# Splitting the next stage's first weights before, rather than after, the last chunk of a feed-forward block

## The reference

```
x = x + 0.5 * swiglu(rmsnorm(x, ffn1_norm), gate1, up1, down1)     # feed-forward, 2816 wide
x = x + concat([mixer(h), memory_cross_attention(h, mem)]) @ w_out  # h = rmsnorm(x, mix_norm)
x = x + 0.5 * swiglu(rmsnorm(x, ffn2_norm), gate2, up2, down2)

def swiglu(h, w_gate, w_up, w_down):
    return (jax.nn.silu(h @ w_gate) * (h @ w_up)) @ w_down
```

## Time and profile before

| | |
|---|---|
| median of three runs | 2265.5 us |
| the profiled execution: its time, its span | 2264.19 us, 2262.4 us |
| PE busy | 1807.7 us (80%) |
| DVE busy | 796.6 us (35%) |
| ACT busy | 604.1 us (27%) |
| HBM read | 601.81 MB, 266 GB/s over the span |

### The profile page before, as it was taken

One profiled execution on the slowest core, in us unless ns is written; L12 is line 12 of the kernel. 1 busy time (PEld: TensorE's weight loads), 2 busy tenths in 40 slices (PEclk: granted clock), 3 DMA queues, 4 the chain that ended last, 5 costly groups with the idle time before them and its releaser, 6 DMA issues.

```text
span 2262.4 us, 29595 instructions
## 1 busy us (share of the span) xinstructions
PE 1807.7 (80%) x12674; PEld 1304.9 (58%) x12674; DVE 796.6 (35%) x906; ACT 604.1 (27%) x709; POOL 143.6 (6%) x140
## 2 busy tenths in 40 slices
PE   4999998999999998899999966655666565656655
PEld 4999895999999996489998831111111111111111
DVE  5556554756666562566656320000000000000001
ACT  5243445433444344544334410000000000000001
POOL 2200001310000000101000120000000000000000
PEclk9999998999999999899999977788888878888787
DMA  5456441555655653045565469999999999999996
GB/s 195 168 167 206 152 149 38 187 168 168 205 185 168 204 164 124 20 145 163 176 206 161 163 274 429 427 429 428 428 429 427 429 428 430 428 429 428 429 429 295
DMA packets 182376, 603.84 MB, mean 267 GB/s; under 512 B 13195, under 2 KB 140438, under 8 KB 157734
## 3 DMA queue, kind: packets, MB, share of 16 engines
q1 hardware_dynamic: 180124, 600.92, 68.4%
q10 hardware_dynamic: 1674, 1.42, 0.2%
q0 software_dynamic: 512, 0.55, 0.1%
HBM read 601.81 MB, written 1.05 MB: 266 GB/s over the span
## 4 chain that ended last, share of the span: by engine, by line
PE 55%; DMA 37%; DVE 4%; ACT 3%; issue 1%; SPq 1%; POOL 0%; ACTq 0%; DVEq 0%; POOLq 0%
PE ps L917 20%; DMA bulk<-in_w_down 19%; DMA bulk<-in_w_up 18%; PE ps L929 11%; PE ps L1079 3%; PE ps L1379 2%; PE ps L902 2%; PE ps L1401 2%; PE ps L982 1%; PE ps L983 1%; PE ps L984 1%; PE ps L1094 1%; PE ps L966 1%; PE ps L992 1%; PE ps L993 1%; PE ps L994 1%
## 5 line engine op out<-in xcount | busy, mean ns | idle before, releaser
L1379 PE MATMUL ps<-bulk 128*32 128x512 f32 x2048 | 320.3, 759 | 217.1 <-DMA bulk<-in_w_up 131.6
L917 PE MATMUL ps<-part,part 128*128 128x256 f32 x3840 | 460.4, 280 | 1.2 <-DVE keep L1994 1.0
L917 PEld LDWEIGHTS ps<-part,part 128*128 128x128 f32 x3840 | 456.0, 189 | 2.1 <-issue 1.4
L1379 PEld LDWEIGHTS ps<-bulk 128*32 128x32 f32 x2048 | 64.0, 125 | 462.4 <-issue 173.8
L1882 DVE TENSOR_TENSOR part<-bulk,part 128x2048 fp32r<-128x2048 f32 x88 | 202.0, 2338 | 248.6 <-ACT part L1459 248.6
L1401 PE MATMUL ps<-bulk 128*32 128x512 f32 x1024 | 171.0, 800 | 107.5 <-DMA bulk<-in_w_down 103.2
L929 PE MATMUL ps<-part,part 128*128 128x256 f32 x2112 | 255.3, 280 | 0.0
L929 PEld LDWEIGHTS ps<-part,part 128*128 128x128 f32 x2112 | 251.6, 189 | 0.0
L1459 ACT ACTIVATE part<-bulk 128x2048 fp32r<-128x2048 f32 x88 | 163.9, 1911 | 263.1 <-DMA bulk<-in_ffn_w_up 263.1
L2327 DVE TENSOR_TENSOR bulk<-bulk,ps 128x512 f32<-128x512 f32 x16 | 11.0, 688 | 602.3 <-PE ps L1379 602.3
L1401 PEld LDWEIGHTS ps<-bulk 128*32 128x32 f32 x1024 | 32.5, 129 | 228.9 <-DMA bulk<-in_w_down 157.9
(11 more groups left out here) (285 smaller groups left out, 2030.2 us busy)
## 6 DMA issues: line engine op xcount, KB each, us to landing
bulk<-in_w_gate SPq DMA_DIRECT2D x64, 2048.0 KB, 26.0
bulk<-in_w_up SPq DMA_DIRECT2D x64, 2048.0 KB, 26.0
bulk<-in_w_down SPq DMA_DIRECT2D x64, 2048.0 KB, 26.2
bulk<-in_ffn_w_gate SPq DMA_DIRECT2D x44, 1024.0 KB, 7.4
bulk<-in_ffn_w_up SPq DMA_DIRECT2D x44, 1024.0 KB, 9.9
bulk<-in_ffn_w_down SPq DMA_DIRECT2D x44, 1024.0 KB, 5.0
bulk<-in_w_out SPq DMA_DIRECT2D x16, 1024.0 KB, 4.9
bulk<-in_gla_w_in SPq DMA_DIRECT2D x14, 1024.0 KB, 5.0
```

The lines of the kernel that those rows point to most:

```text
L917: ins = pe.matmul(y, w_, x_, start=(k == m == 0), stop=(k == KD - 1 and m == 2))
L1379: ins = pe.matmul(ps[j * CAP:(j + 1) * CAP, half, :], xe[:, k, :], w[:, kk, j * HALF:(j + 1) * HALF], start=(k == 0), stop=(k == KD - 1))
```

## The change

In `ffn(f)`, behind chunk 9, ACT and DVE now split the first two weights of the next stage first, and do their part of chunk 10 after it. On ACT one wait is added, on `gate_up(9)`, since the high parts overwrite what it reads (before, the silu of chunk 10 implied it). PE, SP and GpSimd are as before.

```diff
@@ scalar engine, ffn(f), line 1510 @@
                 chunk(NCH - 2, q, gu=False)
-                chunk(NCH - 1, p, gu=False, dn=False)
                 if f == 1:
                     split_gu(2, 0, q)
                 else:
+                    act.wait_ge(gu_used, NCH * (f + 1) - 1)
                     for i in range(2):
                         split_mix((("memkv0", None, "memkv1", "win2")[f], i))
+                chunk(NCH - 1, p, gu=False, dn=False)
```

## The result

| | before | changed |
|---|---|---|
| median | 2265.12 us (4 runs, 2264.19 to 2267.99) | 2284.39 us (4 runs, 2280.78 to 2286.06) |
| profiled execution: time, span | 2264.19, 2262.4 us | 2279.64, 2277.8 us |
| ratio, with its 95% interval | | 1.0081 (1.0063 to 1.0098) |

The changed kernel is slower, as forecast, but by more: 2284 lies just outside the range (2270 to 2283), and 19 us is half as much again as 12. Its profiled execution is faster than all four timed ones.

A forecast was written before the change was run, and what follows sets the result against it. PE alone was taken to bound each block's end, with 96 matmuls back to back; 2264.2 + 9.4 (waits) + 2.8 (clock) = 2276.4 us, 2277.7 by the median. Forecast 2277 us, range 2270 to 2283.

The forecast's parts named there:

- Room of 2.2 us, and nothing waits in the kernel before: Block ends before the change: PE never waits; chunk 10's hidden values are ready 2.2 us before `down(10)` could begin.
- Block 0: landing plus 7.67 us, a wait of 3.6: End of block 0: hidden values ready 7.67 us after the second weight lands, at 225.05 against 221.46; PE waits 3.6 us.
- Blocks 2 and 3, 2.35 and 1.6: Ends of blocks 2 and 3: PE waits 2.35 and 1.6 us for chunk 10's hidden values.
- Block 1, "the first weight was issued before it and is done by then": End of block 1: only the second weight's copy and subtraction follow its landing; PE waits 1.9 us.
- The clock falls in blocks 0 and 2, not in 1 and 3: TensorE's clock halves behind the new waits of blocks 0 and 2 only, 2.8 us in sum.
- the row of 1.87 us: Earlier trace at 891.62: clock stayed 1.00 after 1.87 us idle, so no fall was taken for blocks 1 and 3.
- 1.4 us for a fall: Price per clock fall, from 12 matmuls fewer at 0.118 us each after 2.10 us idle at 978.24.
- The row behind 3.58 us of waiting: Earlier trace: clock 0.50 to about 309.5 after 3.58 us idle, 2.7 us lost; used for the clock's upper bound.
- Nothing is made up later: Stages behind the blocks: all the lost time passes through to the end; the rival that it is made up had 0.08.
- The rival in which the clock falls at all four places: Four block ends: clock falls at each, costing 6.9 us beside 9.4 of waits; 2280.5 us (2281.8 by the median), chance 0.17.
- The sentence named beside it: Trainium skill rule: half speed is the fallback, only activity releases it; taken alone, the clock falls at all four places.
- 9.4 + 2.8: Four block ends: 9.4 us of new PE waiting plus 2.8 us for the clock's falls in blocks 0 and 2.

The follow-up runs named there:

- early loads: Changed kernel with the DMAs of the two weights issued between chunk 10's up and down weights: 2267.02 us, ratio 1.0015 to the kernel before.
- PE kept busy: Changed kernel with 28, 28, 20 and 10 matmuls for nobody on PE between `down(9)` and `down(10)`: 2280.07 us, ratio 1.0085 to the kernel before.
- all but block 1: New order of splits in blocks 0, 2 and 3, block 1 as in the kernel before: 2274.81 us, ratio 1.0058 to the kernel before.
- changed kernel's second trace: Profiled execution of the changed kernel, unaltered, timed again beside the kernel before: median 2288.38 us, ratio 1.0111, span 2283.0 us.

## Why the prediction was wrong, step by step

- *Room of 2.2 us, and nothing waits in the kernel before:* right. The new chain has the DMA, ACT, DVE and PE as described, and early loads took the waits away.
- *Block 0: landing plus 7.67 us, a wait of 3.6:* right. 7.56 measured; the wait was 4.0, since the weight landed 0.3 us later behind its issue and PE started 0.15 us after DVE's end.
- *Blocks 2 and 3, 2.35 and 1.6:* 2.9 and 1.8, since the second weight landed 0.5 and 0.2 us later after the issue of chunk 10's down weight, and by the 0.15 again. The DMA of the second weight landed 11.6 to 13.4 us after the issue of chunk 10's down weight in block 2 of five traces, and 11.0 to 12.2 in block 3. The prediction gave these four landings no spread of their own.
- *Block 1, "the first weight was issued before it and is done by then":* wrong, and the step that failed. `gu_landed` waits on one semaphore for both weights, so the first copy begins when the second weight has landed. The trace of before says so too: ACT's line 1459 is a pair behind one wait for the up weight, as at the end of block 0:

```profile
198.90 3.74 ACT L1459 ACTIVATE part<-bulk 128x2048 fp32r<-128x2048 f32 x2 [7.28 <-DMA bulk<-in_ffn_w_up]
```

  It made the wait 3.9 us instead of 1.9, and put block 1 among those whose clock falls.
- *The clock falls in blocks 0 and 2, not in 1 and 3:* right for 0, 2 and 3, and wrong for 1 because its wait was longer than I had it. For block 3 that was luck: the row of 1.87 us, from which the prediction took that the clock holds behind such waits, is one outcome of two. Behind 1.83 us at this very place it fell (PE kept busy), and behind 1.87 us at a place of the mixer it fell in two later traces.
- *1.4 us for a fall:* mis-sized for blocks 0 and 1. `down(10)` took 2.7, 2.9 and 1.8 us more. In block 2 the price of the fall was about right: 7.42 is 1.5 above the 5.90 of a `down(10)` behind a wait at full clock. In blocks 0 and 1, behind waits of 4 us, the clock was down when the matmuls began and stayed down for another 5.4 and 5.8 us, so that a longer part of them ran at 1.2 GHz than in the fall of the earlier trace rows from which the 1.4 came; they are 2.4 and 2.6 above 5.90. The row behind 3.58 us of waiting, which I had used for the upper bound, was the right one for such a wait. (At 0.118 us each, 5.31 us hold 45 matmuls and not 48, which makes that row 2.4 us and not 2.7.) By size the sum should have been 2.7 + 2.9 + 1.8 = 7.4 and was 2.8.
- *A restart, for which the prediction had no term:* 0.15 us from DVE's end to the first matmul, which is in the waits, and 0.25 us in `down(10)` itself, which is 5.90 us long behind a wait also where the clock held.
- *Nothing is made up later:* about right for blocks 0 to 2: the stages that hold their losses grew by 5.4, 6.1 and 3.8 us where 6.7, 6.7 and 4.6 were lost, and 1.0 of the first 1.3 lies at the start. Of block 3's loss of 2.0 us the changed kernel's first trace has only 0.3 at the projection, and that of all but block 1 only 0.4, where the clock fell once and not twice as in the kernel before; in the changed kernel's second trace 3.3 us are there, with the clock down for longer. So the clock's falls in that stage hide it, and what it costs by itself is not shown.
- *The rival in which the clock falls at all four places* (the prediction calls it the third; it is the second of its list) was right in three of four places. In the fourth, with 1.77 us of idle time, the clock held; with 1.83 us at the same place it fell. By its number, 2280.5 us, it comes nearest to the profiled execution (2279.64), but by another sum: its waits are 3 us too short.
- *The sentence named beside it* (the Trainium skill, "TensorE: Matmul & The Clock Gate", section "What's actually happening", and not "What you observe": half speed is the default, and activity lifts it). That a wait of any length lets the clock fall was my reading of it, and the 1.77 us speak against that.

In sum 9.4 + 2.8 had been forecast at the four places, and 12.5 + 7.5 were there: 3.1 us from the two-weight wait, the landings and the 0.15 us of each restart, 4.7 from the clock and the longer `down(10)` of a restart. What stays open is why the two medians of the changed kernel (2284.39 and 2288.38) lie 5 and 9 us above its first profiled execution. More falls of the clock at other waits would do it, as in the second profiled execution; that is not shown, since the timed ones leave no trace to see it in.

## What to carry to other kernels

Before moving work that waits for a DMA ahead of work on which the busiest engine depends, set the landing of the last of its transfers, plus everything queued behind, against the moment that engine runs out of work. Look at which semaphore is waited for, too: one that counts two transfers makes the first as late as the second. And price a new wait of TensorE by the slow matmuls that follow it, taken from a wait of the same length in the trace: here they cost three fifths as much as the waiting itself (7.5 and 12.5 us).

## What was not expected of the hardware

- Behind some lengths of idle time the clock falls in one execution and not in the next, and no run here shows what decides. At the four places: 1.68, 1.77, 1.79, 1.84 and 1.88 us of idle time without, 1.83 and 1.85 us with a fall; behind 2.34 us and more it fell in all nine cases seen. In the mixers 2.45 us had none, and 1.87 us at one place had one in one trace and none in another. So two executions of one kernel, or two kernels with the same program in a stage, differ there by steps of 1 to 3 us.
- Matmuls with a result that nobody reads can bring time back: 6 us for 52 of them in idle stretches of the kernel before. In the changed kernel they brought the four `down(10)`s back to 5.8 to 6.0 us, but no gain in the total was measured.
